# Split-weight matmuls of a two-block transformer kernel: one 256-column accumulator in place of two 256-column halves

## The chip, the cores and the metric

One core of a Trainium2 chip. The metric is the time of one execution on the device in microseconds; less is better. Before the change three runs gave 2829.0, 2834.8 and 2839.73 us, median 2834.8.

## The reference

Two transformer blocks run one after the other on x of 256 rows (tokens) and width 2048, all in float32. Cut to what matters:

```python
# block one: latent attention and sliding-window attention, then an MLP of width 8192
a = rms_norm(h, attn_norm)
proj = a @ w_in                                  # c_q, c_kv, k_rope, q_s, k_s, v_s
h = h + concat([mla_attention(...), swa_sink_attention(...)]) @ w_out
m = rms_norm(h, mlp_norm)
h = rms_norm(h + square(relu(m @ w_up)) @ w_down, final_norm)
# block two: modulated gating block (branch a) and long convolution (branch b), then an MLP
mod = silu(c) @ w_ada + b_ada                    # sh1, sc1, g1, sh2, sc2, g2
z = (x * (1 + sc1) + sh1) @ w_in + b_in          # z_u, z_v, z_h, z_g
y_a = spatial_gating(gelu(z_u), gelu(z_v), ...) @ w_branch_a
y_b = hyena(z_h, ...) @ w_branch_b
mix = (sigmoid(z_ga) * y_a + sigmoid(z_gb) * y_b) @ w_o + b_o
x = layer_norm(ALPHA * x + g1 * mix)
f = square(relu((x * (1 + sc2) + sh2) @ w_m1 + b_m1)) @ w_m2 + b_m2
x = layer_norm(ALPHA * x + g2 * f)
```

## The kernel before, in words

Activations are held transposed: features on the 128 partitions, the 256 tokens along the free axis. Each float32 operand of a large product is taken apart into a high part, rounded to the engine's float32r format, and a low part, the rest. A product is high x high + high x low + low x high.

All large weights come as one stream of tiles of 128 x 2048 float32 (1 MB), in the order in which they are used: 403 tiles of weights, and 96 tiles of w_ada among them (43 <= tile < 243). The SyncE queue loads them into a ring of four (`stage`, L284, refills at L294). For each weight tile w ScalarE rounds it into `w_hi` (`split`, L758 to L767) and VectorE subtracts to get `w_lo` (`split`, L1113 to L1117); both have two buffers, and the split of tile w + 2 stands in each queue at step w, after TensorE has ended tile w. A tile of w_ada is multiplied by `cond` and summed on VectorE (`condition`, L1388 to L1397), in the slot behind a split.

A tile holds 16 blocks of 128 x 128 weights. On TensorE `tile` (L401) calls `gemm_tile` (L373). A unit is 256 output features, two banks of PSUM of 512 float32, one for each 128 features; two pairs of banks (0, 1 and 2, 3) take turns. Most units are two tiles of eight steps with two blocks each. The moving operand (`xs`, `hs`, `c_q`, `y_a` and so on) is [128, chunk, 512]: columns 0 to 255 are the high part, 256 to 511 the low part. So for one block, the first matmul (L386) has the high weights and all 512 columns: it puts high x high into the lower half of the bank and high x low into the upper half. The second (L390) has the low weights and the 256 high columns and adds into the upper half. In the last step of a unit the two stand in the other order (L393 to L395).

```python
pe.matmul(o2, w_hi[:, wpar, a:a + P], rhs[:, k, :], ...)                     # L386, 512 columns
pe.matmul(o2[:, S:2 * S], w_lo[:, wpar, a:a + P], rhs[:, k, 0:S], ...)       # L390, 256 columns
```

When a unit ends, ScalarE copies the upper halves into `tev` (`take_cross`, L769 to L778, one instruction of 128 x 512), and VectorE adds the lower halves to it (`gather`, L1138 to L1152): one instruction at L1146, or two of 256 with a bias column at L1149. That add frees the banks (`psum_free`), for which TensorE waits before it begins the unit after the next (L376). What is done with `tev` depends on the stage:

- w_in, q_b, kv_b (tiles 0 to 26): multiplied by a norm's factor on VectorE (L1259, L1312). Tiles of q_b and kv_b hold two units each, of four steps.
- w_out (27 to 42): added to `resid` (L1358), with attention in between.
- the MLPs (43 to 170 and 275 to 402), four quarters each of 32 tiles: 16 tiles up, with VectorE relu and square in one instruction (L1413), ScalarE's rounding to `hs` (L959) and VectorE's rest (L1415); then 16 tiles down, added to `resid` (L1425, or with a factor L1422). TensorE waits for the last of `hs` at L592 to L594. Three quarters are a hardware loop, the fourth is written out.
- z (171 to 242), unit i of 36: with bias; for i < 24 ScalarE then takes Gelu or Sigmoid (L992), after a signal of VectorE (L1480); for the rest VectorE makes a three-tap convolution (L1485 to L1489).
- branch a (243 to 250), the long convolution, branch b (251 to 258; L1599 to L1613, each tile a unit of eight steps), w_o (259 to 274; L1621 to L1623).

Between stages are norms: squares on ScalarE (L890, L939, L1081), sums over partitions as float32 matmuls with ones (`stats`, L418 to L421), and the root on VectorE and ScalarE.

The order on every engine is written out by hand; all waits are on semaphores (`lo_ready` for a tile's low part, `tile_done` at a tile's end, `half_done` after the first unit of a q_b or kv_b tile, `evac_done` when a unit's result is made).

## Time and profile before

| what | before |
|---|---|
| runs | 2829.0, 2834.8, 2839.73 us |
| median | 2834.8 us |
| the profiled execution's own time (its span, first to last instruction) | 2835.9 us |
| mean granted TensorE clock | 0.959 |
| instructions | 36999, of them 15134 matmul records and as many weight loads |
| HBM read | 531.22 MB, 188 GB/s over the span |

How to read it: the profile gives a page for one execution (busy time of each engine, the chain of work that ended last, groups of instructions by line) and answers questions on its trace (groups by form, waits, a timeline, sums over windows). PE is TensorE's matmuls, PEld its weight loads, DVE VectorE, ACT ScalarE. The durations of matmuls are modelled and overlap; their starts are what shows the pace. "Idle before" is how long the engine stood before a group's instructions, and the arrow names what ended it. "Issue" means that nothing which the profile shows ended it. Some matmul records are missing.

### The profile page before, as it was taken

How to read it: one execution, taken by the hardware profiler on the slowest of the kernel's cores; microseconds unless marked ns; L12 is line 12 of the kernel's file. 1: busy time of each engine (PE TensorE's matmuls, PEld its weight loads, DVE VectorE, ACT ScalarE, POOL GpSimd, SP SyncE). 2: the span in 40 equal slices, each digit the busy share in tenths (PEclk: the TensorE clock that was granted, in tenths of full speed). 3: DMA queues.
4: the chain of work that ended last, by engine and by line, in shares of the span. 5: the costliest groups of instructions: out<-in, count | busy, mean ns of one | idle time of the engine just before them, and what ended most of it. 6: DMA issues, size and time to landing. Idle time of an engine off the chain costs nothing.

```text
span 2835.9 us, 36999 instructions
## 1 busy us (share of the span) xinstructions
PE 2620.2 (92%) x15134; PEld 2217.3 (78%) x15134; DVE 1793.2 (63%) x1763; ACT 1072.7 (38%) x990; POOL 13.9 (0%) x31
## 2 busy tenths in 40 slices
PE   6997898999999999989999998879799999999996
PEld 5876686888888888868888875457688888888885
DVE  5567466666667676677677984455565555555555
ACT  3254344433434334334434341123334343343432
POOL 0000000000000000000000000000000000000000
PEclk8899799999999999989999998989999999999998
DMA  4233244676666666656777771024335555555541
GB/s 175 93 119 108 73 161 163 238 264 245 248 253 239 261 243 251 235 225 251 268 297 299 297 276 41 4 89 163 134 135 184 187 180 190 181 180 191 179 180 57
DMA packets 76730, 535.66 MB, mean 189 GB/s; under 512 B 8730, under 2 KB 10821, under 8 KB 12576
## 3 DMA queue, kind: packets, MB, share of 16 engines
q1 hardware_dynamic: 74880, 527.74, 50.6%
q0 software_dynamic: 1696, 5.61, 0.6%
q8 instruction: 127, 2.08, 0.3%
q14 instruction: 27, 0.22, 0.0%
HBM read 531.22 MB, written 2.10 MB: 188 GB/s over the span
## 4 chain that ended last, share of the span: by engine, by line
PE 76%; DVE 12%; ACT 6%; issue 5%; DMA 1%; DVEq 0%; SPq 0%; ACTq 0%; POOL 0%
PE ps L386 44%; PE ps L390 22%; ACT w_hi L767 4%; DVE w_lo L1117 3%; PE ps L421 2%; DVE stage L1397 2%; PE ps L701 1%; PE ps L693 1%; PE ps L681 1%; PE ps L523 1%; DVE tev L1146 1%; PE ps L661 1%; DVE tev L1149 0%; DVE tev L1413 0%; DVE vb L1124 0%
## 5 line engine op out<-in xcount | busy, mean ns | idle before, releaser
L386 PE MATMUL ps<-xs,w_hi 128*128 128x512 f32 x4032 | 1447.1, 403 | 85.6 <-DVE w_lo L1117 46.8
L1117 DVE TENSOR_TENSOR w_lo<-stage,w_hi 128x2048 fp32r<-128x2048 f32 x403 | 923.5, 2292 | 794.1 <-ACT w_hi L767 793.2
L767 ACT ACTIVATE w_hi<-stage 128x2048 fp32r<-128x2048 f32 x403 | 771.1, 1913 | 1053.3 <-PE ps L386 687.9
L390 PE MATMUL ps<-xs,w_lo 128*128 128x256 f32 x4032 | 1121.5, 283 | 0.0
L386 PEld LDWEIGHTS ps<-xs,w_hi 128*128 128x128 f32 x4032 | 765.6, 191 | 271.6 <-issue 54.2
L390 PEld LDWEIGHTS ps<-xs,w_lo 128*128 128x128 f32 x4032 | 774.6, 192 | 9.3
L386 PE MATMUL ps<-hs,w_hi 128*128 128x512 f32 x2048 | 719.7, 398 | 12.6 <-DVE hs L1415 12.6
L390 PE MATMUL ps<-hs,w_lo 128*128 128x256 f32 x2048 | 564.0, 281 | 0.0
L386 PEld LDWEIGHTS ps<-hs,w_hi 128*128 128x128 f32 x2048 | 381.2, 188 | 102.0 <-issue 11.3
L390 PEld LDWEIGHTS ps<-hs,w_lo 128*128 128x128 f32 x2048 | 386.6, 189 | 5.7
L1397 DVE SCALAR_TENSOR_TENSOR stage<-stage,cond 128x2048 f32<-128x2048 f32 x96 | 219.4, 2285 | 0.0
L778 ACT ACTIVATE tev<-ps 128x512 f32<-128x512 f32 x220 | 127.4, 579 | 37.2 <-PE ps L386 37.2
L959 ACT ACTIVATE hs<-tev 128x512 fp32r<-128x512 f32 x64 | 40.4, 632 | 229.5 <-DVE tev L1413 229.5
L1146 DVE TENSOR_TENSOR tev<-ps,tev 128x512 f32<-128x512 f32 x144 | 98.5, 684 | 14.8 <-ACT tev L778 14.1
L1415 DVE TENSOR_TENSOR hs<-tev,hs 128x512 fp32r<-128x512 f32 x64 | 44.3, 693 | 44.6 <-ACT hs L959 44.6
L1149 DVE SCALAR_TENSOR_TENSOR tev<-ps,cols,tev 128x256 f32<-128x256 f32 x152 | 66.2, 477 | 1.9 <-ACT tev L778 1.9
L421 PE MATMUL ps<-sq,ones 128*128 128x256 f32 x192 | 50.9, 423 | 12.6 <-ACT sq L1081 5.9
L386 PE MATMUL ps<-y_b,w_hi 128*128 128x512 f32 x128 | 47.3, 409 | 10.5 <-DVE tev L1146 7.9
L421 PEld LDWEIGHTS ps<-sq,ones 128*128 128x128 f32 x192 | 40.4, 213 | 20.5 <-ACT sq L1081 6.7
L386 PE MATMUL ps<-y_a,w_hi 128*128 128x512 f32 x128 | 47.9, 416 | 0.5 <-DVE tev L1146 0.5
L1413 DVE SCALAR_TENSOR_TENSOR tev<-tev 128x512 f32<-128x512 f32 x64 | 44.3, 692 | 2.2
L701 PE MATMUL ps<-idft,y_spec 128*128 128x256 f32 x128 | 33.5, 427 | 11.2 <-DVE y_spec L1567 11.2
(291 smaller groups left out, 1357.7 us busy)
## 6 DMA issues: line engine op xcount, KB each, us to landing
stage<-wstream SPq DMA_DIRECT2D x499, 1024.0 KB, 4.9
resid<-xT SPq DMA_DIRECT2D x4, 512.0 KB, 9.0
out<-resid SPq DMA_DIRECT2D x16, 128.0 KB, 1.9
c_row<-c_row POOLq DMA_DIRECT2D x1, 1024.0 KB, 4.9
w<-w POOLq DMA_DIRECT2D x8, 128.0 KB, 3.0
sgw<-sgw POOLq DMA_DIRECT2D x1, 512.0 KB, 7.7
sgb<-sgb POOLq DMA_DIRECT2D x1, 512.0 KB, 9.0
delta<-delta POOLq DMA_DIRECT2D x1, 512.0 KB, 9.4
```

Source lines behind the costliest of these rows:

```text
L386: return pe.matmul(o2, w_hi[:, wpar, a:a + P], rhs[:, k, :], start=(first and j == 0), stop=stop)
L390: return pe.matmul(o2[:, S:2 * S], w_lo[:, wpar, a:a + P], rhs[:, k, 0:S], start=False, stop=False)
L421: mm = pe.matmul(ps[:, bank, 0:S], ones[:], src[:, i, :], start=(first and i == 0), stop=(last and i == n - 1))
L701: mm = pe.matmul(ps[:, 4 + c // 2, (c % 2) * S:(c % 2) * S + S], y_spec[:, m, c * P:c * P + P], idft[:, m, :], start=(m == 0), stop=(m == 3))
L767: act.activation(w_hi[:, w % 2, :], stage[:, n % RING, :], ACT.Copy).then_inc(hi_ready, 1)
L778: act.activation(tev[:, u % 2], ps[:, b:b + 2, S:2 * S], ACT.Copy).then_inc(cross_ready, 1)
L1117: tt(w_lo[:, w % 2, :], stage[:, n % RING, :], f(w_hi[:, w % 2, :]), ALU.subtract).then_inc(lo_ready, 1)
L1146: tt(t, banks(u, 0), t, ALU.add).then_inc(psum_free, 1)
L1149: ins = stt(t[:, c, :], banks(u, 0)[:, c, :], bias(c), t[:, c, :], ALU.add, ALU.add)
L1397: stt(src, src, 1.0, cond[:], ALU.mult, ALU.mult, accum_out=dst).then_inc(ada_mac, 1)
L1413: stt(t, t, 0.0, t, ALU.max, ALU.mult).then_inc(squared, 1)
L1415: tt(hs[:, 2 * j:2 * j + 2, S:2 * S], t, f(hs[:, 2 * j:2 * j + 2, 0:S]), ALU.subtract).then_inc(evac_done, 1)
```

## The change

Each block is now three matmuls of 256 columns into the lower 256 columns of its bank: high x high, high x low, low x high. The upper half of the banks is unused. Nothing is gathered any more: `take_cross` and `gather` are gone, and what consumed `tev` reads the accumulator in PSUM directly and frees it. `psum_free` becomes two semaphores, one for each pair of banks, and the consumer waits for its own read before it signals `evac_done`. In the first half of a quarter ScalarE takes the relu out of PSUM into `tev` (in the second MLP with the bias, two instructions of 256), and VectorE squares. In the z stage ScalarE adds b_in by the bias of the activation, two instructions of 256 from PSUM; for i >= 24 that is a copy to `tev` for VectorE's convolution. b_o times its factor is folded into the scaling of `resid` (`g1b`).

```diff
+    def acc(u):
+        b = 2 * (u % 2)
+        return ps[:, b:b + 2, 0:S]
+
+    def summed(e, u, w, q=None):
+        if T_QB <= w < T_WOUT and u % 2 == 0:
+            e.wait_ge(sem("half_done"), w - T_QB + 1)
+        else:
+            e.wait_ge(tile_done, w + 1 if q is None else QT * q + w + 1)
...
-            if first and not (isinstance(u, int) and u < 2):
-                pe.wait_ge(psum_free, u - 1)
+            if first and (q is not None or u >= 2):
+                pe.wait_ge(psum_free[upar], u // 2 if q is None else QU // 2 * q + u // 2)
...
-                    o2 = ps[:, 2 * upar + c, :]
+                    o2 = ps[:, 2 * upar + c, 0:S]
...
-                    if last and j == nj - 1:
-                        low()
-                        mm = high(True)
-                    else:
-                        high(False)
-                        mm = low()
+                    hi, lo = w_hi[:, wpar, a:a + P], w_lo[:, wpar, a:a + P]
+                    pe.matmul(o2, hi, rhs[:, k, 0:S], start=(first and j == 0), stop=False)
+                    pe.matmul(o2, hi, rhs[:, k, S:2 * S], start=False, stop=False)
+                    mm = pe.matmul(o2, lo, rhs[:, k, 0:S], start=False, stop=(last and j == nj - 1))
...
-        def take_cross(u, w, q=None):
...
+        def take_relu(u, w, q, second):
+            summed(act, u, w, q)
+            act.wait_ge(evac_done, QU * q + u - 1)
+            if second:
+                for c in range(2):
+                    ins = act.activation(tev[:, u % 2, c], acc(u)[:, c], ACT.Relu,
+                                         bias=col("b_m1", 16 * q + 2 * (u - U_MLP2) + c))
+            else:
+                ins = act.activation(tev[:, u % 2], acc(u), ACT.Relu)
+            ins.then_inc(psum_free[u % 2], 1)
+            act.wait_ge(psum_free[u % 2], QU // 2 * q + u // 2 + 1)
+            act.nop().then_inc(relu_ready, 1)
...
-                take_cross(u, w)
-                if i < 24:
-                    act.wait_ge(sem("z_ready"), i + 1)
...
+                summed(act, u, w)
...
+                else:
+                    act.wait_ge(evac_done, u - 1)
+                    dst, fn = tev[:, u % 2], ACT.Identity
+                for c in range(2):
+                    ins = act.activation(dst[:, c, :], acc(u)[:, c], fn, bias=col("b_in", 2 * i + c))
+                ins.then_inc(psum_free[u % 2], 1)
+                act.wait_ge(psum_free[u % 2], u // 2 + 1)
+                act.nop().then_inc(evac_done if i < 24 else sem("z_ready"), 1)
...
-        def gather(u, q=None, bias=None):
...
+        def took(ins, u, q=None):
+            ins.then_inc(psum_free[u % 2], 1)
+            dve.wait_ge(psum_free[u % 2], u // 2 + 1 if q is None else QU // 2 * q + u // 2 + 1)
+
+        def took_done(ins, u, q=None):
+            took(ins, u, q)
+            dve.nop().then_inc(evac_done, 1)
...
-                t = gather(u)
+                summed(dve, u, w)
                 c = 2 * (u - U_WOUT)
-                tt(resid[:, c:c + 2, :], t, resid[:, c:c + 2, :], ALU.add).then_inc(evac_done, 1)
+                took_done(tt(resid[:, c:c + 2, :], acc(u), resid[:, c:c + 2, :], ALU.add), u)
...
-                        t = gather(u, q, bias)
-                        stt(t, t, 0.0, t, ALU.max, ALU.mult).then_inc(squared, 1)
+                        t = tev[:, u % 2]
+                        dve.wait_ge(relu_ready, QU // 2 * q + ups + j + 1)
+                        tt(t, t, t, ALU.mult).then_inc(squared, 1)
...
-                ts(resid[:, i, :], resid[:, i, :], fold[:, i:i + 1], None, ALU.mult)
+                ts(resid[:, i, :], resid[:, i, :], fold[:, i:i + 1], g1b[:, i:i + 1], ALU.mult, ALU.add)
...
-            link(tt(t, t, gate_b[:, c:c + 2, :], ALU.mult))
+            took(tt(t, acc(u), gate_b[:, c:c + 2, :], ALU.mult), u)
```

The other consumers are changed in the same way as the one at `U_WOUT`.

## Rows read from the trace of the kernel before

**Rows 1.** The page: busy time of each engine, share, instructions

```profile
PE 2620.2 (92%) x15134; PEld 2217.3 (78%) x15134; DVE 1793.2 (63%) x1763; ACT 1072.7 (38%) x990; POOL 13.9 (0%) x31
```

**Rows 2.** The chain that ended last, shares of the span by line

```profile
PE ps L386 44%; PE ps L390 22%; ACT w_hi L767 4%; DVE w_lo L1117 3%; PE ps L421 2%; DVE stage L1397 2%; PE ps L701 1%; PE ps L693 1%; PE ps L681 1%; PE ps L523 1%; DVE tev L1146 1%; PE ps L661 1%; DVE tev L1149 0%; DVE tev L1413 0%; DVE vb L1124 0%
```

**Rows 3.** Second MLP: us, busy us PE, PEld, DVE, ACT, POOL; clock, DMA, GB/s

```profile
2080.00:2800.00 720.00, 711.37 (x4030) 617.70 (x4029) 397.53 (x341) 283.98 (x217) 0.00 (x0) 1.00 0.50 176
```

**Rows 4.** Matmul groups by line and form: busy us, mean ns, idle before, releasers

```profile
L386 PE MATMUL ps<-xs,w_hi 128*128 128x512 f32 x4032 | 1447.1, 403 | 85.6 <-DVE w_lo L1117 46.8 <-DVE xs L1449 22.7 <-DVE xs L1384 8.9
...
L386 PE MATMUL ps<-hs,w_hi 128*128 128x512 f32 x2048 | 719.7, 398 | 12.6 <-DVE hs L1415 12.6
...
L421 PE MATMUL ps<-sq,ones 128*128 128x256 f32 x192 | 50.9, 423 | 12.6 <-ACT sq L1081 5.9 <-ACT sq L939 3.5 <-ACT sq L890 3.2
...
L661 PE MATMUL ps<-w,hid 64*128 64x512 f32 x32 | 20.1, 783 | 5.9 <-ACT k_spec L1036 3.6 <-DVE mixacc L1531 2.2
...
L421 PE MATMUL ps<-resid,ones 128*128 128x256 f32 x64 | 18.3, 437 | 4.8 <-DVE resid L1623 2.5 <-DVE resid L1422 2.3
```

**Rows 5.** Timeline of TensorE, first MLP: start us, us; 16 blocks

```profile
565.49 0.40 PE L386 MATMUL ps<-hs,w_hi 128*128 128x512 f32 x1
...
565.73 0.28 PE L390 MATMUL ps<-hs,w_lo 128*128 128x256 f32 x1
565.73 0.19 PEld L386 LDWEIGHTS ps<-hs,w_hi 128*128 128x128 f32 x1
...
571.15 0.40 PE L386 MATMUL ps<-hs,w_hi 128*128 128x512 f32 x1
```

**Rows 6.** Timeline of TensorE at the end of a unit

```profile
1000.35 0.40 PE L386 MATMUL ps<-hs,w_hi 128*128 128x512 f32 x1
...
1000.59 0.40 PE L390 MATMUL ps<-hs,w_lo 128*128 128x256 f32 x2
...
1000.83 0.40 PE L386 MATMUL ps<-hs,w_hi 128*128 128x512 f32 x1
```

**Rows 7.** Loads of L636, a float32 matmul: min/median/max ns, first, last start

```profile
L636 PEld LDWEIGHTS ps<-sgw,vn_tok x32: 187/192/192, 1358.4 to 1361.9; 128*128 128x128 f32 x32
```

**Rows 8.** ScalarE and VectorE groups by form: busy us, mean ns, idle before

```profile
L778 ACT ACTIVATE tev<-ps 128x512 f32<-128x512 f32 x220 | 127.4, 579 | 37.2 <-PE ps L386 37.2
...
L1117 DVE TENSOR_TENSOR w_lo<-stage,w_hi 128x2048 fp32r<-128x2048 f32 x403 | 923.5, 2292 | 794.1 <-ACT w_hi L767 793.2 <-DVE resid L1652 0.2
...
L1146 DVE TENSOR_TENSOR tev<-ps,tev 128x512 f32<-128x512 f32 x144 | 98.5, 684 | 14.8 <-ACT tev L778 14.1 <-DVE r_kv L1128 0.2 <-DVE k_rope L1293 0.2
L1149 DVE SCALAR_TENSOR_TENSOR tev<-ps,cols,tev 128x256 f32<-128x256 f32 x152 | 66.2, 477 | 1.9 <-ACT tev L778 1.9
```

**Rows 9.** Timeline of VectorE and ScalarE before a w_lo wait, first MLP

```profile
473.21 0.69 DVE L1146 TENSOR_TENSOR tev<-ps,tev 128x512 f32<-128x512 f32 x1
...
473.93 0.69 DVE L1413 SCALAR_TENSOR_TENSOR tev<-tev 128x512 f32<-128x512 f32 x1
...
475.20 1.90 ACT L767 ACTIVATE w_hi<-stage 128x2048 fp32r<-128x2048 f32 x1
...
477.13 2.29 DVE L1117 TENSOR_TENSOR w_lo<-stage,w_hi 128x2048 fp32r<-128x2048 f32 x1 [1.12 <-ACT w_hi L767]
```

**Rows 10.** Waits of TensorE, 460 to 1200 us: us in total, times, longest

```profile
PE ps L386 <- DVE w_lo L1117: 11.7, 8, 1.6
```

**Rows 11.** Waits of TensorE, 1335 to 1500, then 1500 to 1665 us (z stage)

```profile
PE ps L386 <- DVE w_lo L1117: 6.7, 5, 2.5
...
PE ps L386 <- DVE w_lo L1117: 5.5, 5, 1.1
```

**Rows 12.** Timeline of ScalarE in the z stage

```profile
1399.17 0.63 ACT L992 ACTIVATE mixacc<-tev 128x512 f32<-128x512 f32 x1 [4.93 <-DVEq L1480]
```

**Rows 13.** Waits of TensorE, 225 to 292 us (q_b, kv_b), then 1885 to 1932

```profile
PE ps L386 <- DVE tev L1146: 17.0, 9, 3.0
...
PE ps L386 <- DVE tev L1146: 7.9, 5, 1.7
```

More of the change, by code:

```diff
@@ L266, in _program @@
     tile_done = sem("tile_done")
-    cross_ready = sem("cross_ready")
-    psum_free = sem("psum_free")
+    relu_ready = sem("relu_ready")
+    psum_free = [sem(f"psum_free_{i}") for i in range(2)]
     evac_done = sem("evac_done")
@@ L372, in _, with gemm_tile @@
     def _(pe):
[L373 to L376 removed]
+        def gemm_tile(u, q, rhs, k0, nj, first, last, wpar, upar, off, ready):
+            if first and (q is not None or u >= 2):
+                pe.wait_ge(psum_free[upar], u // 2 if q is None else QU // 2 * q + u // 2)
             for j in range(nj):
@@ L1132, in over @@
             return r[:].unsqueeze(1).broadcast_to([P, n, S])
-        def banks(u, half):
-            b = 2 * (u % 2)
-            return ps[:, b:b + 2, half * S:(half + 1) * S]
-        def gather(u, q=None, bias=None):
-            uu = u if q is None else QU * q + u
-            dve.wait_ge(cross_ready, uu + 1)
-            if q is not None or u >= 2:
-                dve.wait_ge(evac_done, uu - 1)
-            t = tev[:, u % 2]
-            if bias is None:
-                tt(t, banks(u, 0), t, ALU.add).then_inc(psum_free, 1)
-            else:
-                for c in range(2):
-                    ins = stt(t[:, c, :], banks(u, 0)[:, c, :], bias(c), t[:, c, :], ALU.add, ALU.add)
-                ins.then_inc(psum_free, 1)
-            dve.wait_ge(psum_free, uu + 1)
-            return t
+        def took(ins, u, q=None):
[4 more added lines that the diff above has]
+            dve.nop().then_inc(evac_done, 1)
         dve.wait_ge(sem("cols_loaded"), 16)
@@ L1246, in _ @@
             if ends:
[L1247 removed]
+                summed(dve, u, w)
+                t = acc(u)
                 i = u - U_IN
@@ L1301, in _ @@
                     split(w + 2)
-                t = gather(u)
+                summed(dve, u, w)
+                t = acc(u)
                 i = u - U_QB
@@ L1417, in mlp_quarter @@
                     else:
-                        t = gather(u, q)
+                        summed(dve, u, t0 + l, q)
+                        t = acc(u)
                         c = 2 * j - QU
@@ L1477, in _ @@
                 i = u - U_Z
-                t = gather(u, None, lambda c: col("b_in", 2 * i + c))
-                if i < 24:
-                    dve.nop().then_inc(sem("z_ready"), 1)
-                else:
+                if i >= 24:
+                    dve.wait_ge(sem("z_ready"), i - 23)
+                    t = tev[:, u % 2]
                     for c in range(2):
@@ L1620, in _ @@
                 c = 2 * (u - U_WO)
-                t = gather(u, None, lambda i: col("b_o", c + i))
+                summed(dve, u, w)
+                t = acc(u)
                 for i in range(2):
```

73 lines of the change are left out of this document (24 added, 49 removed).

## The prediction

> **What bounds the kernel now.** I read first the page's busy times, then the chain that ended last, the matmul groups with the idle time before them, the timeline of the matmuls, and last the waits of TensorE stage by stage. TensorE is busy for 92% of the span against 63% and 38% on VectorE and ScalarE [rows 1]; two thirds of the chain are the two matmuls of the weight blocks, L386 and L390 [rows 2]. In the second MLP it is all but never idle: 711 of 720 us, at the full clock [rows 3]. So two things set the time: how fast the blocks of weights stream, and the short waits between them.
>
> The stream. Durations of matmuls overlap, so I use starts. From 565.49 to 571.15 us 16 blocks went by, 354 ns each, for 512 + 256 columns [rows 5]. Inside, the 512-column one holds the array for 0.24 us and the 256-column one for 0.12. That is in proportion to the columns: 768 columns in 354 ns, so 118 ns for 256. At the end of a unit two 256-column matmuls follow each other, and the wide ones around them start 0.48 us apart: 0.24 + 0.12 + 0.12 [rows 6]. The weight load of each matmul starts with the matmul ahead of it [rows 5], so it is hidden. There are 403 tiles (L1117 runs once for each [rows 8]) of 16 blocks, 6448 blocks, some 2280 us of the 2836.
>
> The waits. What TensorE waits for is listed below with each edit.
>
> **The change, part by part.** *The matmuls.* Columns per block stay 768. Removed: one 512-column matmul with its load; added: two of 256 with a load each, so 6448 more matmuls and as many loads. By columns the block stays at 354 ns. The trace does not show three narrow ones in a row for block after block, so I bound them. Upper end: the narrow pair at the unit's end, 0.12 us each [rows 6], 360 ns, +6 ns a block, +39 us. Lower end: no row has a 256-column matmul quicker than the 128-column ones with a load each in rows 7, 32 in 3.5 us, 113 ns: 339 a block, -15 ns, -97 us. Those have half the columns; the narrow ones of this very stream (0.12) are nearest, and I take 118.5 ns each: +1.5 ns a block, times 6448 = **+10 us**. That loads can come as often as every 0.118 us is in the same row [rows 7].
>
> *Emptying the accumulator.* Before, ScalarE copied the cross half out (L778, 0.58 us), and VectorE added the other (L1146, 0.68; with bias two of 0.48, L1149) [rows 8]. All 220 of both go; the consumer reads the sum itself. Busy time is not the gain (127 us of ScalarE, 165 us of VectorE, mostly beside matmuls): what counts are the waits at whose end a copy or an add stood. The instruction behind a gather starts 0.72 us after it [rows 9]; with bias it is 2 x 0.477 = 0.95.
>
> a) Wait for hs, half-way through each quarter: 12.6 us in 8 waits [rows 4]. ScalarE's split of the next tile (1.9 us) and then VectorE's (2.3) come first, so the copy was already covered; the gather was not. ReLU on ScalarE takes the copy's place and is covered too, even as two biased calls (each at most 0.58, the price for twice the columns). 4 x 0.72 + 4 x 0.95 = -6.7 us.
>
> b) Waits for w_lo in the first MLP: 11.7 us in 8 [rows 10]. A conditioning pass L1397 comes ahead of the gather; L1413 and L1415 follow, ScalarE's next split waits behind its hs copy and starts at 475.20, VectorE's at 477.13 [rows 9]. All of this moves up by the gather: 8 x 0.72 = -5.8 us. The next thing late is the same w_lo, by 0.7 us.
>
> c) The z stage. While i < 24, ScalarE's Gelu or Sigmoid waited up to 5 us for VectorE's bias add, behind a conditioning pass [rows 12], and the next split stood behind it on ScalarE's queue. Now ScalarE needs only the tile: the first five waits, 6.7 us, should go whole. In the last five, 5.5 us, VectorE itself is late with the convolution; it loses a gather of 0.95 each, -4.8 [rows 11]. Together -11.5 us. The residual's scaling gets a second operand in 16 instructions, hidden beside matmuls; were that cover gone, at most 16 x 0.1 = 1.6 us.
>
> d) Branch b: the ring of split, split, mix_lo, gather, two products, copy is longer than a tile; 7.9 us in 5 waits [rows 13]. The gather leaves the ring: 8 tiles x 0.72, less one that starts it, -5.0 us.
>
> e) q_b and kv_b: 17.0 us in 9 waits [rows 13]. The second unit of a tile is freed after both splits and one VectorE instruction of 0.68 us, before and after alike. Only the queues behind it get shorter: -2 us, between 0 and -6.
>
> f) Ends of stages, where the last unit's evacuation lies bare: 3.2 (L890), 3.5 (L939), 2.3 (L1422), 2.5 (L1623), 2.2 (L1531) us [rows 4]. Copy and gather both go: 4 x (0.58 + 0.72) + 0.58 + 0.95 = -6.7 us.
>
> *New waits.* The reader of the accumulator waits for its own end before it signals; behind that wait stand its next instructions, but the gather had the same wait. VectorE now waits for relu_ready or z_ready, signalled some 2.6 us after the tile's end (1.9 + 0.6), when it is still at its split, until 4.2. The DMA queue is moved past nothing: refills hang on w_lo and the conditioning as before.
>
> **Sum.** -6.7 - 5.8 - 11.5 - 5.0 - 2.0 - 6.7 = -37.7; with +10 for the stream, -28. The profiled execution has a span of 2835.9 us, 1.1 above the median of 2834.8. 2835.9 - 28 = 2808, or 2807 against the median. The waits' share could come to -20 (a hidden next releaser) or -45.
>
> **Rivals.** 1) *The third matmul costs something fixed* (the other side). Place: every block; it decides at 37.7 / 6448 = 5.8 ns a block, and from 8 ns the kernel is slower by over 0.5%. For it: rows 6 round to 0.12, which is 2 ns over 118 each, and nothing in the trace has one block's three narrow ones on the same accumulator. Against: spacing goes by columns to a rounding. At 6 ns, 2837; at 9 ns, 2836 - 38 + 58 = 2856. Chance 0.22.
> 2) *Loads do not hide.* Were each load to stand alone for its shown 0.19 us [rows 5], the added 6448 would cost 1225 us: 4023. Rows 5 speak against it: a load starts at the very time of the matmul ahead, and the block takes 354 ns, less than two such loads alone. Chance 0.02. The Trainium skill (TensorE: Matmul & The Clock Gate, the mechanism in Part 3) says that a load overlaps a matmul in flight only when it goes to another row group; by that rule and its figure of 128 / 1.2 = 107 ns (LDWEIGHTS section), an estimate of the added loads would be 690 us. The trace disagrees with that rule: all these loads fill all 128 rows and start with the matmul ahead.
> 3) *The waits stay*, with another releaser just behind the one removed (the DMA, or ScalarE's split). For it: rows 9 have several instructions in one chain; against, DMA is nowhere a releaser of TensorE here. Stream +10, waits -10: 2835. Chance 0.08.
> 4) *The stream gets faster*, some way toward the 113 ns of rows 7. At 4 ns less a block, 2836 - 38 - 26 = 2772. Against: wide and narrow take the same time per column. Chance 0.06.
> That the change does not do what it says has no room: all tiles use the one helper.
>
> **How the numbers follow.** Forecast 2807, chance 0.62, its own range 2785 to 2825. For 8 in 10 I go up into rival 1 to 2850 and down to 2778, part of rival 4. A measurement of this kernel tells some 0.5%, 14 us. Faster by more: nearly all of the forecast, rival 4 and a quarter of rival 1, 0.70. The same: most of rival 3, half of rival 1, and the rest of the forecast, 0.19. Slower: 0.11.
>
> **What would show it.** Right: one line of matmuls of 128x256, three starts a block 0.118 to 0.12 us apart, 16 blocks in 5.66 to 5.72 us; L778, L1146 and L1149 gone; hs waits near 6 us in 8, w_lo waits in the first MLP near 6 and in the z stage's first part near 0; branch b's waits near 4 in all. Wrong: 16 blocks in over 5.8 us (rival 1), loads that no longer start with the matmul ahead (rival 2), wait sums as before under another name (rival 3).

## The result: 0.3% slower, and the profile after

| | before | after |
|---|---|---|
| median of 20 runs | 2829.14 us (2823.34 to 2839.73) | 2837.86 us (2831.39 to 2844.8) |
| ratio | | 1.0027 [1.0017, 1.0037] |
| span of the profiled execution | 2835.9 us | 2833.2 us |
| mean granted TensorE clock | 0.959 | 0.965 |
| matmul records, weight loads | 15134, 15134 | 21582, 21582 |

The forecast was 2807 us, 28 less; the change costs 8.7 us instead. The forecast counted from 2834.8 us, the median of three executions; over twenty the kernel before takes 2829.14. (One profiled execution of each stands on the other side of that difference, 2835.9 and 2833.2 us: single executions differ by more than the change is worth, so the medians decide.) Two of the 13 executions of h1 below, 3714 us at a mean granted clock of 0.645 and 2924 us at 0.842, fell in a slower state of the chip and are left out of its time.

The page of the kernel after: busy time of each engine, and from the chain that ended last the shares by line.

```profile
PE 2661.1 (94%) x21582; PEld 2566.8 (91%) x21582; DVE 1632.4 (58%) x1468; ACT 1021.7 (36%) x914; POOL 13.9 (0%) x31
...
PE ps L398 25%; PE ps L400 24%; PE ps L399 24%; ACT w_hi L768 4%; DVE w_lo L1114 3%; PE ps L422 2%; PE ps L702 1%; PE ps L694 1%; PE ps L682 1%; PE ps L524 1%; DVE stage L1386 1%; PE ps L662 0%; DVE vb L1121 0%; DVE tev L1402 0%; PE ps L457
```

VectorE lost 161 us of work and ScalarE 51 against [rows 1], TensorE has 41 more. The number that moved most is that of the weight loads: 78% of the span before [rows 1], 91% now. The blocks' share of the chain went from 66% [rows 2] to 73%.

The timeline of TensorE in the same stretch as [rows 5]: start us, duration us, engine, line. Sixteen blocks lie between the first row and the last.

```profile
565.22 0.28 PE L398 MATMUL ps<-hs,w_hi 128*128 128x256 f32 x1
565.23 0.19 PEld L399 LDWEIGHTS ps<-hs,w_hi 128*128 128x128 f32 x1
565.34 0.28 PE L399 MATMUL ps<-hs,w_hi 128*128 128x256 f32 x1
565.35 0.19 PEld L400 LDWEIGHTS ps<-hs,w_lo 128*128 128x128 f32 x1
565.46 0.28 PE L400 MATMUL ps<-hs,w_lo 128*128 128x256 f32 x1
...
570.98 0.28 PE L398 MATMUL ps<-hs,w_hi 128*128 128x256 f32 x1
```

Sixteen blocks take 5.76 us, 360 ns each, and the starts in this stretch are 0.12 us apart. Over all 6448 blocks the median from one low product to the next is 360 ns (worked out from the starts in the trace), where it was 349 before, with a mean of 352. In the old block the wide matmul takes 230 to 241 ns to the next start and the narrow one 113 to 120, and whole tiles went by at mostly one of two paces, some 347 or some 354 ns a block (353 in the median tile); the stretch of [rows 5] is one of the slower kind. What decides between the two is open. A load still starts with the matmul ahead.

The matmul groups by line and form: busy us, mean ns | idle before, releasers. They answer to [rows 4].

```profile
L398 PE MATMUL ps<-xs,w_hi 128*128 128x256 f32 x4032 | 1160.6, 288 | 66.2 <-DVE w_lo L1114 23.6 <-DVE xs L1440 23.0 <-DVE xs L1373 10.5
...
L422 PE MATMUL ps<-sq,ones 128*128 128x256 f32 x192 | 48.3, 407 | 11.5 <-ACT sq L1078 7.0 <-ACT sq L936 2.6 <-ACT sq L890 1.9
```

The waits of TensorE over the whole span (us in total, times, longest), the ones that the steps of the prediction and the sum below rest on:

```profile
PE ps L398 <- DVE w_lo L1114: 23.6, 12, 16.0
...
PE ps L398 <- issue: 7.5, 5, 1.8
...
PE ps L398 <- DVE hs L1404: 5.1, 8, 0.6
PE ps L466 <- ACT q_swa L837: 4.4, 7, 1.7
...
PE ps L398 <- DVE v_feat L1301: 3.4, 2, 2.1
...
PE ps L398 <- DVE tev L1603: 3.2, 5, 0.7
PE ps L398 <- DVE q_rope L1301: 3.2, 2, 2.1
PE ps L398 <- DVE q_nope L1301: 3.1, 2, 2.4
...
PE ps L398 <- DVE c_raw L1247: 2.1, 1, 2.1
PE ps L422 <- DVEq L1139: 2.1, 2, 1.0
...
PE ps L398 <- DVE k_nope L1301: 1.3, 1, 1.3
PE ps L662 <- DVEq L1139: 0.9, 1, 0.9
```

And of its waits for w_lo in two windows, from 460 to 1200 us and from 1335 to 1500 us, which answer to [rows 10] and the first of [rows 11]; from 1500 to 1665 us TensorE has none:

```profile
PE ps L398 <- DVE w_lo L1114: 4.0, 8, 0.5
...
PE ps L398 <- DVE w_lo L1114: 1.1, 1, 1.1
```

So the waits did go, about as listed, and the stream ate them. Times by stage, each worked out from the trace as the distance from the first matmul with w_lo in a stage to the first in the next, and for the second MLP to the end of its last (e1 and e2 are the experiments below; the profiled execution of e2 took 2790.84 us, 12.8 above its median):

| us | before | e1 | e2 | after |
|---|---|---|---|---|
| w_in (tiles 0 to 19) | 207.9 | 209.7 | 208.4 | 208.6 |
| q_b, kv_b | 73.4 | 74.1 | 70.7 | 68.9 |
| attention, w_out | 155.2 | 156.9 | 153.2 | 153.8 |
| first MLP | 768.5 | 787.7 | 759.1 | 777.9 |
| z | 442.2 | 448.1 | 428.5 | 436.5 |
| branch a, long convolution | 208.2 | 208.3 | 203.0 | 204.4 |
| branch b | 59.9 | 59.9 | 55.5 | 55.5 |
| w_o | 126.0 | 128.7 | 122.9 | 126.2 |
| second MLP | 742.1 | 757.7 | 736.1 | 754.2 |

Where most of the blocks are, in the two MLPs, the kernel after is 9.4 and 12.1 us slower; in z, both branches and q_b it is faster, by 5.7, 8.2 and 4.5 us.

### The profile page after: what moved, and what is told of

Read it like the earlier page. It is cut to its first block, busy times and chain, and to the rows that moved or that the text cites. A ratio compares the mean times of both kernels' runs of the same rounds, so it can differ in the third digit from the quotient of the medians.

```text
span 2833.2 us, 49318 instructions
## 1 busy us (share of the span) xinstructions
PE 2661.1 (94%) x21582; PEld 2566.8 (91%) x21582; DVE 1632.4 (58%) x1468; ACT 1021.7 (36%) x914; POOL 13.9 (0%) x31
## 4 chain that ended last, share of the span: by engine, by line
PE 82%; DVE 10%; ACT 5%; issue 3%; DMA 1%; DVEq 0%; SPq 0%; POOL 0%; ACTq 0%
PE ps L398 25%; PE ps L400 24%; PE ps L399 24%; ACT w_hi L768 4%; DVE w_lo L1114 3%; PE ps L422 2%; PE ps L702 1%; PE ps L694 1%; PE ps L682 1%; PE ps L524 1%; DVE stage L1386 1%; PE ps L662 0%; DVE vb L1121 0%; DVE tev L1402 0%; PE ps L457 0%
## 5 line engine op out<-in xcount | busy, mean ns | idle before, releaser
L398 PE MATMUL ps<-xs,w_hi 128*128 128x256 f32 x4032 | 1160.6, 288 | 66.2 <-DVE w_lo L1114 23.6
L399 PE MATMUL ps<-xs,w_hi 128*128 128x256 f32 x4032 | 1153.0, 286 | 0.0
L400 PE MATMUL ps<-xs,w_lo 128*128 128x256 f32 x4032 | 1152.6, 286 | 0.0
L398 PEld LDWEIGHTS ps<-xs,w_hi 128*128 128x128 f32 x4032 | 786.8, 195 | 73.0 <-issue 48.0
L399 PEld LDWEIGHTS ps<-xs,w_hi 128*128 128x128 f32 x4032 | 786.9, 195 | 0.3
L400 PEld LDWEIGHTS ps<-xs,w_lo 128*128 128x128 f32 x4032 | 786.0, 195 | 0.0
L398 PE MATMUL ps<-hs,w_hi 128*128 128x256 f32 x2048 | 581.7, 284 | 5.1 <-DVE hs L1404 5.1
L399 PE MATMUL ps<-hs,w_hi 128*128 128x256 f32 x2048 | 579.8, 283 | 0.0
L400 PE MATMUL ps<-hs,w_lo 128*128 128x256 f32 x2048 | 579.8, 283 | 0.0
L398 PEld LDWEIGHTS ps<-hs,w_hi 128*128 128x128 f32 x2048 | 393.2, 192 | 6.9 <-issue 5.0
L399 PEld LDWEIGHTS ps<-hs,w_hi 128*128 128x128 f32 x2048 | 393.2, 192 | 0.2
L400 PEld LDWEIGHTS ps<-hs,w_lo 128*128 128x128 f32 x2048 | 393.2, 192 | 0.0
L422 PE MATMUL ps<-sq,ones 128*128 128x256 f32 x192 | 48.3, 407 | 11.5 <-ACT sq L1078 7.0
L702 PEld LDWEIGHTS ps<-idft,y_spec 128*128 128x128 f32 x128 | 27.6, 218 | 18.3 <-DVE y_spec L1556 12.9
L1402 DVE TENSOR_TENSOR tev<-tev 128x512 f32<-128x512 f32 x64 | 43.8, 684 | 0.0
```

What stands on the lines that cost most here:

```text
L398: pe.matmul(o2, hi, rhs[:, k, 0:S], start=(first and j == 0), stop=False)
L399: pe.matmul(o2, hi, rhs[:, k, S:2 * S], start=False, stop=False)
L400: mm = pe.matmul(o2, lo, rhs[:, k, 0:S], start=False, stop=(last and j == nj - 1))
L422: mm = pe.matmul(ps[:, bank, 0:S], ones[:], src[:, i, :], start=(first and i == 0), stop=(last and i == n - 1))
L702: mm = pe.matmul(ps[:, 4 + c // 2, (c % 2) * S:(c % 2) * S + S], y_spec[:, m, c * P:c * P + P], idft[:, m, :], start=(m == 0), stop=(m == 3))
L1402: tt(t, t, t, ALU.mult).then_inc(squared, 1)
```

## The experiments

With the trace of after read, the theory was that a narrow matmul start costs a fixed 120 ns, above its share of the columns, and that the stream lost there what the waits gave. Its rivals: the time went into new waits, or into accumulating three times on the same 256 columns of a bank. When these had fallen, the question became what sets the 120 ns, the columns or the weight load. The expectations below were written before each run. Ratios and times of before are those of runs on the same chip as the experiment; the 2837.86 us of after stand beside 2829.14 us of before on theirs. The ablations e3 and e5 to e8 ran once each.

### The two halves of the change, each alone: e1 and e2

e1 is the kernel before with the wide matmul cut in two; copy and gather stay.

```diff
-                        return pe.matmul(o2, w_hi[:, wpar, a:a + P], rhs[:, k, :], start=(first and j == 0),
+                        pe.matmul(o2[:, 0:S], w_hi[:, wpar, a:a + P], rhs[:, k, 0:S], start=(first and j == 0),
+                                  stop=False)
+                        return pe.matmul(o2[:, S:2 * S], w_hi[:, wpar, a:a + P], rhs[:, k, S:2 * S], start=False,
                                          stop=stop)
```

> The kernel before with its halves, copy and gather kept, only the 512-column matmul taken apart into two of 256 (the second still into the upper half). Theory F (a narrow matmul has a fixed part: 120 ns for 256 columns, about 231 for 512, so a block costs 360 instead of 352 ns): +7 to +8 ns in 6448 blocks is +45 to +52 us, less a few us because a longer tile shortens the waits: 2868 to 2880, ratio 1.014 to 1.018 to before; all three matmuls start 0.120 us apart. Rival E (the stream costs nothing, the direct reading of PSUM costs what the gather saved): 2829, ratio 1.000.

e2 is the kernel after with the stream of before. The cross products are computed into the upper half and nobody reads them, so they are missing from the output; the work of TensorE is that of before, that of the other engines is that of after.

```diff
-                    pe.matmul(o2, hi, rhs[:, k, 0:S], start=(first and j == 0), stop=False)
-                    pe.matmul(o2, hi, rhs[:, k, S:2 * S], start=False, stop=False)
-                    mm = pe.matmul(o2, lo, rhs[:, k, 0:S], start=False, stop=(last and j == nj - 1))
+                    both = ps[:, 2 * upar + c, :]
...
+                        pe.matmul(both, hi, rhs[:, k, :], start=(first and j == 0), stop=False)
+                        mm = pe.matmul(both[:, S:2 * S], lo, rhs[:, k, 0:S], start=False, stop=False)
```

> The changed kernel with the 512- and the 256-column matmul back; the consumers still read the lower half alone, so the two cross products are summed but left out of the result. Theory F: the stream is as before and the evacuation as after: 2829 less the 35 to 40 us of shorter waits is 2790 to 2796, ratio 0.986 to 0.989. Rival E: nothing to gain from the evacuation, 2829 to 2838, ratio 1.000 to 1.003. The two together should add up: (e1 - before) + (e2 - before) = after - before, +9 us, under both.

| stream | with copy and gather | read straight from PSUM |
|---|---|---|
| 512 + 256 columns | before: 2828.62 us | e2: 2778.0 us, ratio 0.9807 [0.9783, 0.9831] |
| 3 x 256 columns | e1: 2883.39 us, ratio 1.0187 [1.0162, 1.0211] | after: 2837.86 us |

The timeline of e1 at 1000 us, where the halves are still two places in the bank:

```profile
1000.01 0.28 PE L386 MATMUL ps<-hs,w_hi 128*128 128x256 f32 x1
1000.13 0.28 PE L388 MATMUL ps<-hs,w_hi 128*128 128x256 f32 x1
1000.25 0.28 PE L392 MATMUL ps<-hs,w_lo 128*128 128x256 f32 x1
```

and of e2 in the first MLP:

```profile
565.18 0.28 PE L405 MATMUL ps<-hs,w_lo 128*128 128x256 f32 x1
565.30 0.39 PE L404 MATMUL ps<-hs,w_hi 128*128 128x512 f32 x1
565.53 0.28 PE L405 MATMUL ps<-hs,w_lo 128*128 128x256 f32 x1
```

Both parts of the change do something large, in opposite directions. The narrow stream costs 54.8 us with the gather (e1 against before) and 59.9 us without it (after against e2): 8.5 and 9.3 ns for each of the 6448 blocks. Reading the sum from PSUM gains 50.6 us with the wide stream and 45.5 us with the narrow one. Both came out larger than expected (2868 to 2880 us for e1, 2790 to 2796 for e2), and they do not quite add up: 54.8 - 50.6 is +4, where the whole change is +9. With the slower stream there are fewer waits to save: TensorE's waits for w_lo from 460 to 1200 us are 11.7 us before and 9.8 in e1, 5.7 in e2 and 4.0 after. The starts in e1 are 0.12 us apart with the three products in two places, so adding three times on one place is not needed for it. New waits are out too: e2 and after have the same consumers, and differ by the stream alone.

### Columns or something else: e3 and e5

e3 takes half of the columns away from the middle product alone (high x low is then left out for 128 of the 256 tokens).

```diff
-                    pe.matmul(o2, hi, rhs[:, k, S:2 * S], start=False, stop=False)
+                    pe.matmul(o2[:, 0:P], hi, rhs[:, k, S:S + P], start=False, stop=False)
```

> The changed kernel with the middle of the three matmuls of a block over 128 columns instead of 256 (high x low is left out for half of the tokens). Theory F with a part by columns and a fixed part (9 ns + 0.433 ns a column): the next matmul starts 65 ns after the middle one instead of 120, a block takes 305 ns, and the kernel gets 250 to 350 us faster, to 2490 to 2590, where VectorE's and ScalarE's chains allow it. Rival L (a weight load is good for one start every 113 to 120 ns whatever the columns): the middle one keeps 113 to 120 ns and the time stays within 45 us of 2838.

It ran in 2796.78 us, 41 less than after. The timeline, with three of the weight loads:

```profile
565.30 0.28 PE L398 MATMUL ps<-hs,w_hi 128*128 128x256 f32 x1
...
565.42 0.22 PE L399 MATMUL ps<-hs,w_hi 128*128 128x128 f32 x1
565.42 0.19 PEld L400 LDWEIGHTS ps<-hs,w_lo 128*128 128x128 f32 x1
565.48 0.33 PE L400 MATMUL ps<-hs,w_lo 128*128 128x256 f32 x1
565.53 0.19 PEld L398 LDWEIGHTS ps<-hs,w_hi 128*128 128x128 f32 x1
565.65 0.28 PE L398 MATMUL ps<-hs,w_hi 128*128 128x256 f32 x1
565.65 0.19 PEld L399 LDWEIGHTS ps<-hs,w_hi 128*128 128x128 f32 x1
```

The matmul behind the 128-column one starts 0.06 us after it, as half of 0.12 would have it. But that next one then holds until 0.17 us have gone by. A block takes 351 ns at the median instead of 360, for 640 columns instead of 768: a sixth of the columns is gone, 60 ns of the 360, and 9 came out (41 us over the kernel are 6.4 a block). Something that comes three times a block and does not depend on the columns holds the block up. What comes three times a block is the weight load, and its rows show it: while the matmuls start 0.06 and 0.17 us after one another, the loads keep starting 0.11 and 0.12 us apart. The load for L398 no longer starts with the matmul ahead (565.48) but 0.05 us later, 0.11 us after the load before it, and its matmul starts 0.12 us behind it.

e5 gives both matmuls of a block 512 columns. The lower half then holds high x high and low x high; high x low, and a low x low that the kernel never had, go to the upper half, which is not read, so high x low is missing from the output.

```diff
-                    pe.matmul(o2, hi, rhs[:, k, 0:S], start=(first and j == 0), stop=False)
-                    pe.matmul(o2, hi, rhs[:, k, S:2 * S], start=False, stop=False)
-                    mm = pe.matmul(o2, lo, rhs[:, k, 0:S], start=False, stop=(last and j == nj - 1))
+                    both = ps[:, 2 * upar + c, :]
+                    pe.matmul(both, hi, rhs[:, k, :], start=(first and j == 0), stop=False)
+                    mm = pe.matmul(both, lo, rhs[:, k, :], start=False, stop=(last and j == nj - 1))
```

> The changed kernel with two matmuls of 512 columns a block (high and low weights each over all 512 columns, into the whole bank; the lower half read by the consumers now lacks high x low and holds low x high, the upper half is left out). Theory F: 231 ns a start, 462 a block, +102 ns over 360: about 2838 + 640 = 3480 (waits for splits vanish beside longer tiles, so 3440 to 3490). By columns alone, at 120 ns for each 256: 480 a block, 3590. By the 235 ns which the trace of before has between a wide and a narrow start: 470 a block, 3530.

It ran in 3374.85 us, under all that was expected (3440 to 3590). Sixteen blocks lie between the first and the last of these rows of its timeline:

```profile
565.09 0.39 PE L399 MATMUL ps<-xs,w_hi 128*128 128x512 f32 x1
565.32 0.39 PE L400 MATMUL ps<-xs,w_lo 128*128 128x512 f32 x1
...
572.34 0.39 PE L399 MATMUL ps<-xs,w_hi 128*128 128x512 f32 x1
```

7.25 us for 16 blocks of 1024 columns: 453 ns a block, 0.4425 ns a column, 227 ns for 512 columns with a load at every start. By columns alone 256 would then take 113 ns. So in the kernel after each narrow matmul holds the array some 6.5 ns longer than its columns ask for; three times that is the 20 ns between 360 and the 340 that 768 columns would take.

### The load by itself: e6, e7, e8

e6 cuts all three products to 128 columns (except in a unit's first step; for the upper 128 tokens the rest is left out). With the columns halved, they should ask for some 57 ns a matmul by e5, and the load, if it is the load, sets the pace.

```diff
+                    n = S if first and j == 0 else P
-                    pe.matmul(o2, hi, rhs[:, k, 0:S], start=(first and j == 0), stop=False)
+                    pe.matmul(o2[:, 0:n], hi, rhs[:, k, 0:n], start=(first and j == 0), stop=False)
...
```

> The changed kernel with all three matmuls of a block over 128 columns (but in a unit's first step); half of the tokens keep only their first step's sum. Theory L, formed on the last runs (three starts need three weight loads, and a float32r load is good for one start in 117 to 120 ns, with one start of slack): a block still takes 350 to 360 ns, 2790 to 2840. By columns (theory F): 3 x 65 = 195 ns a block, hundreds of us less, until the chain of ScalarE's and VectorE's splits bounds a tile at some 4.3 us, about 2300.

Its time, 4113.95 us where 2790 to 2840 were expected, is that of another clock: the mean granted clock of the run is 0.596. So it is read by windows. Columns are: window, its length, busy us (count) of PE, PEld, DVE, ACT and POOL, granted clock, DMA share, GB/s; the second fence is its timeline at 440 us, in the first window, and at 1000 us, where the granted clock is 0.50 as in the second.

```profile
440.00:460.00 20.00, 20.00 (x176) 19.90 (x176) 12.79 (x7) 7.48 (x5) 0.00 (x0) 1.00 0.40 154
...
600.00:700.00 100.00, 100.00 (x471) 100.00 (x471) 36.56 (x25) 23.56 (x18) 0.00 (x0) 0.50 0.35 128
```

```profile
440.03 0.27 PE L401 MATMUL ps<-xs,w_lo 128*128 128x128 f32 x1
440.14 0.28 PE L399 MATMUL ps<-xs,w_hi 128*128 128x128 f32 x1
440.25 0.28 PE L400 MATMUL ps<-xs,w_hi 128*128 128x128 f32 x1
...
1000.23 0.41 PE L401 MATMUL ps<-xs,w_lo 128*128 128x128 f32 x1
1000.44 0.41 PE L399 MATMUL ps<-xs,w_hi 128*128 128x128 f32 x1
```

At a granted clock of 1.00 (2.4 GHz) the starts are 0.11 us apart (176 in 20 us; most single ones 111 or 112 ns), at 0.50 (1.2 GHz) they are 0.21 apart (471 in 100 us, 212 ns). In e3 a single 128-column matmul among longer ones held its successor up for 0.06 us; here, where all are that short, it is 0.11 at the same clock, for half the columns of after. Columns do not set that, and e3 has a start after 0.06 us, so no fixed least distance between two matmuls does either. The load is what is left: about 112 ns for 128 columns of weights.

e7 goes the other way: all 256 columns of tokens, and 64 columns of weights a load instead of 128 (except in a unit's first and last step; otherwise half of the output features are left out).

```diff
+                    m = P if first and j == 0 or last and j == nj - 1 else 64
-                    pe.matmul(o2, hi, rhs[:, k, 0:S], start=(first and j == 0), stop=False)
+                    pe.matmul(o2[0:m], hi[:, 0:m], rhs[:, k, 0:S], start=(first and j == 0), stop=False)
...
```

> The changed kernel with 64 instead of 128 weight columns in each load (but in a unit's first and last step), 256 moving columns as they are; the upper 64 features of each block are left out in the other steps. Theory L: the load is what sets 120 ns, and with half of it the moving columns bound, at half of the 227 ns that a 512-column start took: 3 x 114 = 341 ns, -19 ns in about 5600 blocks, -105 us: 2730. If 120 ns is a fixed part of each matmul beside its columns, the block stays at 360 and the time at 2838.

It ran in 2740.11 us. Its timeline, again 16 blocks:

```profile
565.76 0.28 PE L399 MATMUL ps<-hs,w_hi 128*64 128x256 f32 x1
565.87 0.28 PE L400 MATMUL ps<-hs,w_hi 128*64 128x256 f32 x1
565.99 0.28 PE L401 MATMUL ps<-hs,w_lo 128*64 128x256 f32 x1
...
571.20 0.28 PE L399 MATMUL ps<-hs,w_hi 128*64 128x256 f32 x1
```

5.44 us for 16 blocks, 340 ns, 113 a start: with the load made short the narrow matmul takes exactly what its columns ask for by e5. Same moving columns, same columns of PSUM, same order, as many loads and matmuls, half the weight columns, 98 us less: the time that the weight load takes holds up the stream of after, and not a fixed cost of a matmul. (Half as many rows of PSUM are written too, which this run does not take apart. But e5 writes all rows at 0.4425 ns a column, 113 ns for 256, so the writing does not ask for 120.)

e8 asks whether the two add up or whether the longer one wins: full loads, 192 columns in each product (for the last 64 tokens all but the first step is left out). Against e6:

```diff
-                    n = S if first and j == 0 else P
+                    n = S if first and j == 0 else 192
```

> The changed kernel with all three matmuls of a block over 192 columns instead of 256 (but in a unit's first step; the last 64 tokens keep only their first step's sum). Halving the load gave 114 ns a start, halving the columns 112: load and columns alone are each good for some 112 to 114 ns, and together they take 120. If it is the tie of the two that costs the 6 to 8 ns, 192 columns are clear of it: 112 ns a start at the full clock, 336 a block. If the extra grows with the columns beside the load, 116: 348 a block. At a steady clock of 0.96 that is 2690 or 2770 us; as fewer columns can cost the granted clock, the starts at the full clock decide, not the time.

2723.98 us. Its timeline:

```profile
565.24 0.27 PE L399 MATMUL ps<-hs,w_hi 128*128 128x192 f32 x1
565.34 0.28 PE L400 MATMUL ps<-hs,w_hi 128*128 128x192 f32 x1
565.46 0.27 PE L401 MATMUL ps<-hs,w_lo 128*128 128x192 f32 x1
...
569.92 0.27 PE L399 MATMUL ps<-hs,w_hi 128*128 128x192 f32 x1
```

From 565.24 to 569.92 are 14 blocks, 334 ns each; over the whole run most of the single starts are 110 to 114 ns apart, median 111. That is the pace of e6, though the columns went from 128 to 192. Side by side, at full clock:

| run | columns of tokens | columns of weights a load | ns from start to start |
|---|---|---|---|
| e6 | 128 | 128 | 111 to 112 |
| e8 | 192 | 128 | 111 to 112 |
| e7 | 256 | 64 | 113 to 114 |
| e1, after | 256 | 128 | 120 |
| e5 | 512 | 128 | 227 |

Among these even streams the longer one wins in every row but one. Where the load (112) and the columns (113.5) are all but equal, the pace is 120, over either, and shortening either of them for all three matmuls takes the whole excess away.

The mixed streams fit less well. The block of before has loads for 2 x 112 = 224 ns and columns for 340, and takes 349 at the median; that of e3 has 336 and 283, and takes 351. So the excess is not only a matter of two sums that tie: it is there in each kernel that has 256-column matmuls beside full loads, at 9 to 20 ns a block, and in none of the others (e5, e7, e8). What the change added is the step from 349 or 352 to 360. Why load and columns lose time beside each other is open: no run here looks inside that.

### What to do with it: h1, h2, h3

The wide pair saves 9 ns a block, reading PSUM directly saves waits. Which is worth more differs by stage, so a kernel can take each where it pays. h1 is the kernel after with the pair of 512 and 256 columns in 68 units whose consumer only adds to `resid` (5 of w_out, 7 of w_o, 7 of the 8 down units in each quarter of both MLPs). There VectorE adds both halves straight from PSUM, one add more and no copy.

```diff
+    def wide(w):
+        l = (w - T_MLP1) % QT if T_MLP1 <= w < T_Z else (w - T_MLP2) % QT if w >= T_MLP2 else -1
+        return (T_WOUT + 4 <= w < T_MLP1 - 2 or T_WO <= w < T_MLP2 - 2 or 16 <= l < 30)
...
+        def add_halves(make, u, n, q=None):
+            make(acc(u)).then_inc(sem("half_added"), 1)
+            dve.wait_ge(sem("half_added"), n + 1)
+            took_done(make(crossed(u)), u, q)
```

> The changed kernel, with the 512- and the 256-column matmul back in the units that are only added to the residual and whose end nobody waits for (5 of w_out, 7 of w_o, 7 in each of 8 quarters on the way down: 68 units of 32 blocks, 2176 blocks); VectorE adds the lower and then the upper half to the residual, both from PSUM, no copy. By the two runs before (the direct version is 60 us longer with narrow than with wide matmuls, 9.3 ns in each of 6448 blocks) that is -20 us against the changed kernel: 2818, ratio 0.996 to before (0.993 to 0.998). If the second add makes VectorE late for the next split, the gain is lost in waits for w_lo: 2838.

2819.91 us, ratio to before 0.9965 [0.9952, 0.9979]; 18 us under after, for 68 x 32 = 2176 blocks, 8.2 ns each.

h2 adds the first seven up units of each quarter of the second MLP, with copy and gather as before: 28 units, 896 blocks. Against h1:

```diff
-        return (T_WOUT + 4 <= w < T_MLP1 - 2 or T_WO <= w < T_MLP2 - 2 or 16 <= l < 30)
+        return (T_WOUT + 4 <= w < T_MLP1 - 2 or T_WO <= w < T_MLP2 - 2 or 16 <= l < 30 or w >= T_MLP2 and 0 <= l < 14)
...
-                        take_relu(u0 + j, t0 + l, q, t0 == T_MLP2)
+                        if wide(t0 + l):
...
+                            act.activation(tev[:, j % 2], crossed(j), ACT.Copy).then_inc(sem("cross_ready"), 1)
```

> As the one before, and wide matmuls also in the first seven units up of each quarter of the second MLP, there with ScalarE's copy and VectorE's gather as in the kernel before (28 units, 896 blocks more). Another -8 us: 2810, ratio 0.993 (0.991 to 0.996). If the copy and the gather bring waits into the second MLP, it is not below the one before.

2815.11 us, ratio 0.994 [0.9918, 0.9961]: by the medians another 5 us where 8 were expected, and the two intervals just overlap. h3 does the same in the first MLP; against h2:

```diff
-        return (T_WOUT + 4 <= w < T_MLP1 - 2 or T_WO <= w < T_MLP2 - 2 or 16 <= l < 30 or w >= T_MLP2 and 0 <= l < 14)
+        return (T_WOUT + 4 <= w < T_MLP1 - 2 or T_WO <= w < T_MLP2 - 2 or 16 <= l < 30 or 0 <= l < 14)
```

> As h2_wide_up_too, and wide matmuls with copy and gather also in the first seven units up of each quarter of the first MLP (28 units, 896 blocks more). The stream gives 896 x 9 ns = -8 us; the gather is back in the chain that ends in the 8 waits for w_lo of the first MLP (0.5 us each in the changed kernel, 1.4 in the one before), +6 us: 2813, ratio 0.993 to 0.995. If those waits stay at 0.5 us, 2807.

2815.73 us, ratio 0.9948 [0.9927, 0.9968]: nothing more. The waits of TensorE for w_lo between 460 and 1200 us, of h2 and then of h3:

```profile
PE ps L416 <- DVE w_lo L1138: 4.0, 8, 0.5
```

```profile
PE ps L413 <- DVE w_lo L1138: 12.1, 8, 1.6
```

In the first MLP the conditioning passes on VectorE come ahead of the gather, and with the gather the eight waits of [rows 10] are back, 8.1 us more; 896 blocks at 9 ns are the same 8 us. By the stage sums the first MLP takes 771.0 us in h2 and 772.4 in h3. In the second MLP no conditioning stands there. TensorE waits there for hs 3.0 us where it is 2.6 after, and for w_lo once, 2.8 us for 2.3, and the stage takes 741.4 us for 754.2 after, 7 ns for each of its 1792 wide blocks. So h2 is the version to keep of those tried: 0.6% under before, and 0.8% under the change.

## Why the prediction was wrong

It said "faster", and the result is within 0.5% on the other side, inside the outer range of 2778 to 2850 us but by way of rival 1. Its steps, one by one:

**The stream: the step that failed.** "I take 118.5 ns each: +1.5 ns a block, times 6448 = +10 us." Measured +8.5 to 9.3 ns a block, +55 to +60 us. The term was mis-sized for two reasons. First, the bounds were right and the choice between them was not: the upper end, 0.12 us from the pair at a unit's end [rows 6], was the true value, and the text went under it because 118 is a third of 354. That third took for granted what was in question, that time goes by columns. The row that spoke against it was in the text: the matmuls of [rows 7] came 113 ns apart with 128 columns each, hardly faster than 256 columns at 118. They were taken for a lower bound; that half the columns saved almost nothing is the sign of a load that sets the pace (those are float32 and not float32r; that the same holds for this stream was shown only by e6 and e8). Second, 354 ns is one stretch of 16 blocks; over all blocks the mean was 352 and the median 349. The upper end with the mean block would have given 8 x 6448 = +52 us.

**Why it is so.** The text held that the load is hidden because it starts with the matmul ahead. It does so after the change as well. What starts early may still end late: three loads of 112 ns and three lots of columns of 113.5 ns run beside each other, and a block that needs 340 ns at most of either takes 360. The block of before had two loads in 352 ns, one of them beside 512 columns with time to spare; the change spent that. The Trainium skill (TensorE: Matmul & The Clock Gate, "Back-to-back issue gap") says that in a stream of loads and matmuls both set the spacing of the starts. The runs bear that out: the pace is that of the load in e6 and e8 and that of the columns in e5 and e7. By the Trainium skill's figure for a load, 1.2 columns a nanosecond (same page, "LDWEIGHTS (loading the stationary operand)"), 128 columns take an estimated 107 ns. e6 and e8 show 111 to 112.

The busy share of the loads was no more than a hint. The Trainium skill (Perfetto Trace Analysis, "Identifying the Most-Contended Engine") has the reader judge how near TensorE is to its limit by the share of the peak arithmetic rate that it reaches and by the busy share of its weight loads, not by that of its matmuls. Here the loads' share went from 78% to 91% while the matmuls' went from 92% to 94%, and 78% [rows 1] times 21582 / 15134 loads is 111%, more than a span holds; the prediction did not do that sum. But it gives no price, since the records of loads overlap, and the share does not tell a stream held by loads from one that is not: e8, held by them, shows 89%, and e7, whose pace is that of the columns, 90%.

**The waits: right.** By the rows above against those of before. The last column is e2, which has the new consumers and the stream of before:

| step | forecast us | after us | e2 us |
|---|---|---|---|
| a) hs, 12.6 [rows 4] to 5.1; 6.0 in e2 | -6.7 | -7.5 | -6.6 |
| b) w_lo in the first MLP, 11.7 [rows 10] to 4.0; 5.7 | -5.8 | -7.7 | -6.0 |
| c) z stage, 6.7 + 5.5 [rows 11] to 1.1; 1.2 | -11.5 | -11.1 | -11.0 |
| d) branch b, 7.9 [rows 13] to 3.2; 4.0 | -5.0 | -4.7 | -3.9 |
| e) q_b and kv_b, 17.0 [rows 13] to 13.1 (five rows, c_raw to k_nope); 13.0 | -2.0 | -3.9 | -4.0 |
| f) ends of stages: 3.2, 3.5, 2.5 + 2.3 and 2.2 [rows 4] to 1.9, 2.6, 2.1 and 0.9; 7.7 in all in e2 | -6.7 | -6.2 | -6.0 |
| sum | -37.7 | -41.1 | -37.5 |

The waits of e2 for hs, for `tev` in branch b and, from 460 to 1200 us, for w_lo:

```profile
PE ps L404 <- DVE hs L1409: 6.0, 8, 0.8
PE ps L404 <- DVE tev L1608: 4.0, 5, 0.9
```

```profile
PE ps L404 <- DVE w_lo L1119: 5.7, 8, 0.7
```

So on the stream for which they were worked out the steps sum to what was forecast; that the sum is exact is in part luck, since single steps are off by up to 2 us, to either side. Step b) is exact to the next thing late, w_lo itself by 0.7 us. That the waits of after are shorter still is the work of the slower stream.

Outside the list, the other waits for w_lo lost 4.4 us (46.8 [rows 4] to 23.6 in all, less b and c) and attention's wait for q_swa 2.5 (6.9 before), while `issue`, in five places where one stretch of code passes to the next, grew by 2.7 us (4.8 before), and some waits at stage ends grew by 1 to 2 us each. By the pages all of TensorE's idle time fell from 215.7 to 172.1 us, 43.6 less. The runs put the whole gain of the direct reading at 45.5 to 50.6 us. The copy and the gather are gone from the groups, and in z and the first MLP what stood behind them is on time. Of the new waits, that of VectorE for its own read shows in TensorE's list at three stage ends, as the instruction behind it (L1139, 2.1 and 0.9 us), where 7.0 us of waits for the longer chain stood before.

**The rivals.** Rival 1, a fixed cost of the third matmul, is what happened in its size, at 9 ns a block; the text gave it 0.22 and 2856 us. The place, the sign and the size were right; the cause is not a fixed cost of a matmul, since e7 has as many of them at 113 ns, but the load beside it. The result is 18 us lower because the text counted from 2835.9 us and not from the 2829.14 of twenty executions (7 us), and because the waits gave more than 37.7. Where it decides was drawn right too: at 5.8 ns a block with a gain of 37.7, and at 7.1 to 7.8 with the gain measured. "Against: spacing goes by columns to a rounding" was no argument, since a rounding of 0.01 us on three starts is worth more than the whole forecast (5 ns x 3 x 6448 = 97 us). Rival 2, loads alone, did not occur: a block of three loads that show 0.19 us each takes 0.36. Rival 3, waits under another name, did not occur. Rival 4, a faster stream, needs a shorter load: e7 is that kernel.

**What would show it.** "16 blocks in 5.66 to 5.72 us" right, "over 5.8" wrong: it came to 5.76, in the gap between, which is where a step of 0.04 us over 16 blocks (2.5 ns a block) is worth 16 us over the kernel. The hs waits (5.1 for "near 6"), branch b (3.2 for "near 4") and z (1.1 for "near 0") were as said, w_lo in the first MLP lower (4.0 for "near 6"; e2 has 5.7).

## What to carry to other kernels

A matmul's weight load that starts early is not free: ask how long the columns beside it run, and count loads and columns of a block as two separate sums. The larger of the two is a lower bound and not yet the price: with 256-column matmuls beside full loads the blocks here took 349 for 340, 351 for 336 and 360 for 340 ns. Keep moving operands wide enough that one load has slack.

When a change trades the stream against waits, make both halves alone (here -51 and +55 us, together +9 because a slower stream leaves fewer waits to save) before judging the sum; the mixed kernel, wide where the consumer can take two halves and direct where a wait stood, was faster than either kernel.

Take a per-block price from starts over thousands of blocks, not from one stretch of 16 rounded to 0.01 us. And when a row shows half the columns at almost the same distance, as [rows 7] did, ask what sets that distance before using it as a bound.

## What the runs showed of the hardware that was not expected

- A load of 128 columns of float32r weights sets a floor of 111 to 112 ns between starts in an even stream at a granted clock of 1.00 (e6, e8) and of 212 ns at 0.50 (e6). With 64 columns of weights it no longer shows under 256 columns of tokens (e7, 113 to 114 ns).
- Load and columns that tie cost more than either: 120 ns for 112 and 113.5. Without a tie there is still an excess where 256 columns and full loads mix with other lengths: 349 ns for 340 before, 351 for 336 in e3.
- Among 256-column matmuls a 128-column one lets the next start after 0.06 us, and that next one holds for 0.17 us (e3), while the loads go on at 0.11 to 0.12 us: the sum of a block moves by 9 ns, not by 60.
- The busy share of the weight loads is 89% in a stream held by them (e8) and 90% in one that goes by its columns with loads of half the size (e7).
- e6 got a mean clock of 0.596, with 0.50 over whole windows in which TensorE was busy throughout; e8 and after, with longer matmuls, got 0.956 and 0.965. It is one execution, and one of h1, with 256 and 512 columns, got 0.645; so whether the short matmuls of e6 brought its clock about is open.
